# A hybrid decoder step with expert retrieval: POOL's bursts of u gathers one burst further ahead, slots in groups of two, causal key blocks, stages placed by weight

## What is computed

```python
D_MODEL, SEQ, DEC_BATCH, PAST_LEN, PAGE_SIZE = 1024, 1024, 8, 2048, 128
N_HEADS, KV_RANK, QK_ROPE, PEER_HEADS, PEER_KEYS, PEER_TOPK = 4, 256, 64, 8, 128, 16

def latent_attention(q_lat, q_rope, ckv, kr, mask):
    s = (einsum('bqhr,bkr->bhqk', q_lat, ckv) + einsum('bqhp,bkp->bhqk', q_rope, kr)) * SM_SCALE
    s = where(mask, s, -inf)                      # prompt: kpos <= qpos
    return einsum('bhqk,bkr->bqhr', softmax(s), ckv)

def peer_block(x, w_query, sub_keys, expert_u, expert_v):
    q = (x @ w_query).reshape(t, 8, 2, 128)
    s = einsum('thcd,ckd->thck', q, sub_keys)
    sv, si = top_k(s, 16)
    cand = sv[:, :, 0, :, None] + sv[:, :, 1, None, :]
    top_s, pos = top_k(cand.reshape(t, 8, 256), 16)
    experts = take(si0 * 128 + si1, pos)          # 8 x 16 = 128 experts for each token
    a = gelu(einsum('td,thkd->thk', x, expert_u[experts]))
    return einsum('thk,thkd->td', softmax(top_s) * a, expert_v[experts])
```

## Time and profile before

| | us |
|---|---|
| median of 3 runs (3758.39 to 3769.8) | 3765.8 |
| the profiled execution | 3753.85 |
| its span, first to last instruction | 3751.9 |
| first gather | 256.5 |
| tiles 0 to 6 (first u gather to the next tile's) | 403 to 416 |
| last tile, to its last v gather | 545 |

### The profile page before, as it was taken

The page is one execution under the profiler, slowest core; times in us unless marked ns, Lnnn a source line. Parts: engine busy times, 40 slices in busy tenths (PEclk is TensorE's granted clock), DMA queues, the critical chain, the costliest instruction groups (busy, mean ns, idle before and its releaser), DMA issues.

```text
span 3751.9 us, 47864 instructions
## 1 busy us (share of the span) xinstructions
...
## 2 busy tenths in 40 slices
...
GB/s 182 67 161 412 368 401 391 367 400 358 411 359 411 355 404 362 396 372 401 409 348 410 363 411 349 408 361 382 384 376 393 379 409 370 330 331 313 311 308 163
DMA packets 371757, 1321.00 MB, mean 352 GB/s; under 512 B 59684, under 2 KB 78670, under 8 KB 348424
## 3 DMA queue, kind: packets, MB, share of 16 engines
...
...
## 4 chain that ended last, share of the span: by engine, by line
PE 32%; DVE 32%; DMA 14%; issue 12%; ACT 6%; POOL 2%; SPq 1%; DVEq 1%; ACTq 0%; POOLq 0%
DVE u_ring L1310 12%; PE acc L684 11%; DMA v_ring<-in_expert_v,pick_cur 7%; PE front L410 5%; DMA u_ring<-in_expert_u,pick_cur 4%; PE front L517 3%; PE front L566 3%; PE front L538 2%; ACT diag L933 2%; DVE sv L1201 2%; PE front L518 2%; DVE si_u L1202 2%; DVE work L1201 1%; DMA w_ring<-in_w_pieces 1%; DVE work L1202 1%
## 5 line engine op out<-in xcount | busy, mean ns | idle before, releaser
L1448 POOL DMA_INDIRECT v_ring<-in_expert_v,pick_cur x1024 | 1206.2, 1178 | 687.3 <-PE acc L684 422.4
L684 PE MATMUL acc<-v_ring,diag 128*64 128x512 f32 x4096 | 1188.3, 728 | 592.4 <-ACT diag L933 419.3
L1448 POOL DMA_INDIRECT u_ring<-in_expert_u,pick_cur x1024 | 1106.7, 1081 | 666.2 <-issue 290.5
L1310 DVE CUSTOM_DVE_ANT_0 u_ring<-u_ring,xn_cur 128x1024 f32<-128x1024 f32 x1024 | 1210.6, 1223 | 268.8 <-DMA u_ring<-in_expert_u,pick_cur 253.7
L684 PEld LDWEIGHTS acc<-v_ring,diag 128*64 128x64 f32 x4096 | 348.9, 164 | 1269.2 <-issue 686.6
L410 PE MATMUL front<-work,w_ring 128*128 128x128 f32 (+1 forms) x4896 | 607.2, 283 | 7.0 <-DVE work L1194 5.6
L410 PEld LDWEIGHTS front<-work,w_ring 128*128 128x128 f32 x4896 | 593.0, 201 | 41.6 <-issue 32.6
L926 ACT ACTIVATE gelu<-dots 128x4 f32<-128x4 f32 x256 | 52.7, 206 | 1834.2 <-DVE dots L1310 1833.4
L933 ACT ACTIVATE diag<-ident,wgt 128x64 f32<-128x64 f32 x1024 | 271.5, 336 | 120.7 <-DVE wgt L1316 120.7
L566 PE MATMUL front<-w_ring,work 128*128 128x256 f32 (+1 forms) x576 | 149.7, 426 | 75.5 <-DVE work L1169 65.9
L566 PEld LDWEIGHTS front<-w_ring,work 128*128 128x128 f32 (+1 forms) x576 | 116.2, 205 | 113.3 <-issue 64.2
...
## 6 DMA issues: line engine op xcount, KB each, us to landing
...
u_ring<-in_expert_u,pick_cur POOLq DMA_INDIRECT x1024, 12.3
v_ring<-in_expert_v,pick_cur POOLq DMA_INDIRECT x1024, 10.7
...
```

Of the source, the lines that this page charges most:

```text
L684: last = nc.tensor.matmul(acc[rows, half, :], diag[:, s % RING, :], v_ring[:, s % RING, half * 512:half * 512 + 512], start=False, stop=(s ...
L1310: v.tensor_tensor_reduce(u_ring[:, slot, :], u_ring[:, slot, :], xn2_cur[:, block_of(r), :], 1.0, 0.0, ALU.mult, ALU.add, dots[:, g * G + ...
L1448: pool.indirect_dma_start(ring[:, slot, :], None, a[table][0], bass.IndirectOffsetOnAxis(ap=pick, axis=0)).then_inc(loaded[slot], 16)
```

## The change

Slots go in groups of two (G = 2, 64 groups; rings stay at 8 slots). DVE's dots and ACT's gelus run AHEAD = 2 groups ahead, four slots as before. POOL has its own bursts of 4 and issues u of burst k+2 ahead of v of burst k, over the tiles' borders. For that, selects come in parts: for tiles 1 to 7 heads 0 to 3 and 4 to 7, for tile 0 heads 0 and 1, 2 and 3, 4 to 7. Each part's picks and gates are moved at its end, except a tile's last, which is moved where before. In tile 0 only the first part stands ahead of the first gather; six queries and two selects go beside its expert part.

A table of weights (COST) places the stages: over the first 60 groups of a prompt tile, 62 of the last. Stages with several pieces of weights are split into one stage a piece. In tile 1's plan, the queries stand in groups 37 to 55, the selects in 46 and 57, and every second or third group from 17 on has no stage.

Attention covers only key blocks 0 to f in tile f. All Fori loops are unrolled; the zeroing of the key tiles by POOL is gone.

The diff, cut to its core:

```diff
...
-G = 4
+G = 2
 GROUPS = SLOTS // G
-RING = 2 * G
+RING = 8
+AHEAD = 2
+BURST = 4
 HB = P // 2
...
+def parts_of(f):
+    return [(0, 2), (2, 4), (4, 8)] if f == 0 else [(0, 4), (4, 8)]
+def parts_done(f, part):
+    return sum(len(parts_of(e)) for e in range(f)) + part
...
+_FIRST = (["norm", "turn"] + [("latent", k) for k in range(3)] + ["latent_norm"] + [("z_in", k) for k in range(2)] + ["kv_rows"]
+          + [("z_gate", k) for k in range(2)] + [("conv", k) for k in range(2)] + ["q_proj", "q_latent"])
+_MIX = ["attn", "mix_norm"] + [("mix_out", k) for k in range(N_OUT)] + ["ffn_norm", "ffn_turn", ("query", 0)]
+COST = {"norm": 0.5, "turn": 0.3, "latent": 0.5, "latent_norm": 0.8, "z_in": 0.7, "kv_rows": 0.2, "z_gate": 0.7, "conv": 0.8, "q_proj": 0.6,
...
+def _part(f, part):
+    h0, h1 = parts_of(f)[part]
+    return [("query", h + 1) for h in range(h0, h1)] + [("select", part)]
+def front_of(f):
+    return _named(_FIRST + [("head", h) for h in range(H + 1)] + _MIX + _part(f, 0))
+def rest_of(f):
+    return sum([_part(f, part) for part in range(1, len(parts_of(f)))], [])
+def place(stages, span):
+    total, done, groups = sum(COST[s[2]] for s in stages), 0.0, [[] for g in range(GROUPS)]
+    for s in stages:
+        groups[min(int(done * span / total), span - 1)].append(s)
+        done += COST[s[2]]
+    return groups
+def plan(it):
+    if it < TILES - 1:
+        stages = [(0, P) + s for s in rest_of(0)] if it == 0 else []
+        return place(stages + [(it + 1, P) + s for s in front_of(it + 1) + rest_of(it + 1)], GROUPS - 4)
+    f = it + 1
+    stages = _named(_FIRST + [("pages", n) for n in range(SB * QUARTERS + QUARTERS)] + _MIX) + _part(f, 0) + rest_of(f)
+    return place([(f, SB) + s for s in stages], GROUPS - 2)
+PLAN = [plan(it) for it in range(TILES)]
...
+def key_blocks(f, half):
+    return min(4, max(0, f + 1 - 4 * half))
...
+                    ks = slice(half * 512, half * 512 + key_blocks(f, half) * P)
+                    if ks.stop == ks.start:
+                        continue
+                    dst = F[half][:, 0:ks.stop - ks.start]
                     for c in range(2):
-                        nc.tensor.matmul(F[half][:, :], q_lat[:, c, h, :], ckvT[:, c, ks], start=(c == 0), stop=False)
-                    last = nc.tensor.matmul(F[half][:, :], q_ro[:, h, :], krT[:, ks], start=False, stop=True)
+                        nc.tensor.matmul(dst, q_lat[:, c, h, :], ckvT[:, c, ks], start=(c == 0), stop=False)
+                    last = nc.tensor.matmul(dst, q_ro[:, h, :], krT[:, ks], start=False, stop=True)
...
+                    for j in range(f + 1):
                         last = nc.tensor.matmul(F[4][:, c * P:(c + 1) * P], ckv_rows[:, j, c * P:(c + 1) * P],
-                                                W[1][:, j * P:(j + 1) * P], start=(j == 0), stop=(j == TILES - 1))
+                                                W[1][:, j * P:(j + 1) * P], start=(j == 0), stop=(j == f))
...
             def tile(it, T):
-                for g in range(GROUPS):
-                    stages = beside(g, T)
-                    before = 1 if has_pages(stages) else len(stages)
-                    for name, n in stages[:before]:
-                        stage(it + 1, T, name, n)
...
             def diag_group(it, g):
                 act.wait_ge(on.w_made, it * GROUPS + g + 1)
-                act.wait_ge(on.v_free, RING + it * SLOTS + (g - 1) * G)
+                act.wait_ge(on.v_free, it * SLOTS + (g + 1) * G)
...
+                for g in range(AHEAD + 1):
+                    gelu_group(it, g)
...
+                keys = W[0][:, 0:(f + 1) * P]
                 for half in range(2):
-                    last = v.scalar_tensor_tensor(out=W[0][:, half * 512:half * 512 + 512], in0=low_keys[:],
-                                                  scalar=small_col(C_LIM + half), in1=F[half][:, :], op0=ALU.add, op1=ALU.min)
+                    w = key_blocks(f, half) * P
+                    if w:
+                        last = v.scalar_tensor_tensor(out=W[0][:, half * 512:half * 512 + w], in0=low_keys[:, 0:w],
+                                                      scalar=small_col(C_LIM + half), in1=F[half][:, 0:w], op0=ALU.add, op1=ALU.min)
...
+            def move_gates(f, part):
+                h0, h1 = parts_of(f)[part]
+                after(dve, on.w_made, (f - 1) * GROUPS + h1 * TOPK // G if f else 0)
+                return spread_blocks(gate_cur, gate_next, h0 * TOPK // 2, h1 * TOPK // 2)
+            def move_picks(f, part):
+                h0, h1 = parts_of(f)[part]
+                after(dve, on.v_free, RING + (f - 1) * SLOTS + h1 * TOPK if f else 0)
+                spread_blocks(pick_cur, pick_next, h0 * TOPK // 2, h1 * TOPK // 2).then_inc(on.picks_moved, 1)
...
+                if T == P and (f == 0 or part < len(parts_of(f)) - 1):
+                    assert f == 0 or weighed[0] >= (f - 1) * GROUPS + hs.stop * TOPK // G
+                    own(move_gates(f, part))
+                    move_picks(f, part)
...
             def dot_group(it, g, first=0, end=G):
                 for r in range(first, end):
-                    slot = (g % 2) * G + r
-                    dve.wait_ge(u_loaded[slot], (it * (GROUPS // 2) + g // 2 + 1) * 16)
+                    s = g * G + r
+                    slot = s % RING
+                    dve.wait_ge(u_loaded[slot], (it * (SLOTS // RING) + s // RING + 1) * 16)
...
             def move_on(own, f):
-                if not isinstance(f, int):
-                    dve.wait_ge(on.w_made, f * GROUPS)
+                if f:
+                    own(move_gates(f, len(parts_of(f)) - 1))
                     dve.wait_ge(on.u_free, f * SLOTS + RING)
-                own(spread_blocks(gate_cur, gate_next, 0, HB))
                 for i in range(2):
...
+                for g, stages in enumerate(PLAN[it]):
+                    if g and g + AHEAD < GROUPS:
+                        dot_group(it, g + AHEAD)
                     if g:
                         weigh_group(it, g)
-                    before = 1 if has_pages(stages) else len(stages)
-                    for name, n in stages[:before]:
-                        stage(own, it + 1, T, name, n)
-                    if g and g + 1 < GROUPS:
-                        dot_group(it, g + 1, half, G)
-                    for name, n in stages[before:]:
-                        stage(own, it + 1, T, name, n)
+                    for s in stages:
+                        stage(own, *s)
                 if T == P:
-                    own.check(DVE_FRONT)
-                own2 = Own(dve, on.dve_peer, it * DVE_PEER + DVE_MOVE)
-                if T == P:
-                    move_on(own2, it + 1)
+                    move_on(own, it + 1)
                     dot_group(it + 1, 0)
                     total_square(it, P)
-                    dot_group(it + 1, 1)
+                    for g in range(1, AHEAD + 1):
+                        dot_group(it + 1, g)
                     weigh_group(it + 1, 0)
-                    finalize(own2, it, P)
-                    move_picks(it + 1)
-                    own2.check(DVE_PEER)
+                    finalize(own, it, P)
+                    move_picks(it + 1, len(parts_of(it + 1)) - 1)
                 else:
...
                     last.then_inc(on.state_kept, 1)
-            front.check(DVE_FRONT)
-            move_on(Own(dve, on.dve_peer, 0), 0)
-            move_picks(0)
+            move_on(own, 0)
             dot_group(0, 0)
-            dot_group(0, 1)
+            for g in range(1, AHEAD + 1):
+                dot_group(0, g)
             weigh_group(0, 0)
-            with dve.Fori(0, TILES - 1) as it:
+            for it in range(TILES - 1):
                 tile(it, P)
             tile(TILES - 1, SB)
-            own = Own(dve, on.dve_tail, 0)
...
-            pool.memset(ckv_rows[:], 0.0).then_inc(on.zeroed, 1)
-            pool.memset(ckvT[:], 0.0).then_inc(on.zeroed, 1)
-            pool.memset(krT[:], 0.0).then_inc(on.zeroed, 1)
...
-            def gather_group(it, g, table, ring, loaded):
-                if g * G == SLOTS // 2:
-                    pool.wait_ge(on.picks_moved, it + 1)
-                for s in range(g * G, (g + 1) * G):
+            def gather_burst(it, first, table, ring, loaded):
+                for part, (h0, h1) in enumerate(parts_of(it)):
+                    if first == h0 * TOPK:
+                        pool.wait_ge(on.picks_moved, parts_done(it, part + 1))
+                for s in range(first, first + BURST):
                     if table == "expert_u":
                         pool.wait_ge(on.u_free, it * SLOTS + s + 1)
...
                     waited(pool)
                     gather(table, ring, s % RING, loaded, pick_cur[:, s:s + 1])
-            def tile(it):
-                pool.wait_ge(on.picked_moved, it + 1)
-                gather_group(it, 0, "expert_u", u_ring, u_loaded)
```

(14 more changed lines are left out.)

282 lines of the change are left out of this document (124 added, 158 removed).

## The result

The changed kernel takes 4228.7 us, the median of 4 runs (4219.1 to 4235.3); the kernel before takes 3763.0. The ratio is 1.123, with a 95% interval of 1.121 to 1.126. The prediction was 3640 us, faster: wrong in sign, and 589 us off.

A forecast was written before the change was run, and what follows sets the result against it. DMA transfers, with a ceiling of 411 GB/s, were taken as the bound. Start -88, tile 0 +16, seven tiles -37, last tile -17 give -126: from 3753.9 to 3628, as a median 3640 us; range 3530 to 3735.

The forecast's parts named there:

- The start: Before the first gather: one-block attention saves 35 us, fewer queries and selects 53; first gather 88 us sooner (75 to 92).
- Tile 0: Six queries, two selects and their weights now stand beside tile 0: 16 us given back, up to 30.
- One burst further ahead: Gather order in tiles: DVE's wait for u goes, v is asked for later; costs 3 us a tile (0 to 21).
- Groups of two: In each tile: 32 more weighings on DVE, 5 us, and as many gelus on ACT; beside the work, nothing.
- Causal blocks: Attention in tiles 1 to 7: three eighths of its work goes, saving 4.3 us a tile (0 to 8).
- The change of tiles: Between tiles: first twelve u gathers wait only for free slots, loops gone; 4 of 10.4 us given back (0 to 10).
- The last tile: Last tile: weight pieces as own stages with v work between, 12 us, tile's beginning 5; saves 17 (0 to 50).
- (d): Rival: v comes too late in every zone; tiles of 433 us, 3838 us in all; chance 0.06.
- (b): Rival: order inside the tiles changes nothing, only the start gains; -82 us, 3684 in all; chance 0.17.
- (c): Rival: POOL's own pace, gathers lengthened beside DVE operations reading two tiles; tiles grow by 5 us, 3712 in all; chance 0.12.
- (a): Rival: tiles reach nearly the transfer ceiling, 388 us, DVE never starving; 3510 us in all; chance 0.25.

The follow-up runs named there:

- w1: lead1 with weighings and diagonals one group ahead and dots and gelus three groups ahead: 3636.2 us, 0.968 of the kernel before.
- g4lead1: The changed kernel with slots in groups of four again and u gathers one burst ahead, not two: 3663.8 us, 0.976 of the kernel before.
- lead1: The changed kernel with only u gathers put one burst ahead of v instead of two, groups of two kept: 3848.7 us, 1.024 of the kernel before.
- g4full: g4lead1 with attention of tiles 1 to 7 over all eight key blocks, key tiles zeroed by POOL: 3747.6 us, 0.996 of the kernel before.
- g4lead2: The changed kernel with slots in groups of four again, the lead of two bursts kept: 3803.4 us, 1.010 of the kernel before.

## Why the prediction was wrong

**What bounds the kernel** was read rightly, and the sum still failed: transfers were the limit before, at 384 GB/s, and I took for granted that they stay it. They stay it only as long as the rings are full of issued gathers. The landing time in the earlier trace rows (10.7 us against 4.7 with an empty queue) was that reserve; I used it as a range for a latency, not as the stock that the change could eat.

**The start**: right. The first gather comes at 160.1 us (forecast 168). Attention of tile 0, from its first score matmul to the first with w_uv as in the forecast's 54.9, takes 85.02 - 67.13 = 17.9 us (forecast 20), and from the end of the second query to the first gather there are 160.14 - 151.51 = 8.6 (forecast 9):

```profile
67.13 0.71 PE L557 MATMUL front<-ckvT,rows_next 128*128 128x128 f32 x4 [1.16 <-ACT rows_next L910]
...
85.02 3.78 PE L590 MATMUL front<-mo,w_uv 128*128 128x128 f32 x16 [0.46 <-ACT mo L924]
...
151.51 0.19 DVE L1294 TENSOR_TENSOR gate_next<-work 128x32 f32<-128x32 f32 x1
...
160.14 1.43 POOL L1469 DMA_INDIRECT u_ring<-in_expert_u,pick_cur  x1 [159.68 <-DVE pick_cur L1260]
```

It is -96.4 where the sum had -88. Most of the difference is that attention itself begins 7.9 us sooner (67.13 against 75.02), for which the sum had no term.

**Tile 0**: 16 us, up to 30, were to be given back beside what the other tiles do. That was too little. Before, tile 0 was 8.1 us shorter than tiles 1 to 6 (402.9 against 411.0); in the changed kernel it is 11.6 us longer than they are, so it gave back 19.7. By the same working it is 24.1 in w1, 29.6 in g4lead1, 37.1 in lead1 and 47.2 in g4full. Which of the stages beside tile 0 holds it up was not measured.

**One burst further ahead**: the step that failed most. Its loop had the right members (dots, issues, landing, PE, stage), and its sentence that v is asked for one burst later was the right one. What failed is the cover: 20.5 us of transfers for two rounds were set against a loop of 23 to 29, as if all sixteen slots could be in flight. By the count above, with dots only four slots ahead of PE's use the lead leaves 2 to 4 v slots issued, so the loop would run once for each burst, in every zone, and not in six pairs of one. I took 3 us a tile and gave 0 to 21; it is 52 (lead1 against the changed kernel), 380 us of the whole time. That DVE's wait for u would go was right, 33.4 to 13.5, and worth nothing. "The queue shortens itself when this loop binds" was true as well: landing fell to 6.7, and the loop still bound.

**Groups of two**: "beside the work, nothing" counted 32 weighings of 0.16 us and forgot what a group is in this order: the number of slots weighed before DVE goes into a stage. It is 29 us a tile (lead1 against g4lead1), 185 us of the whole, and w1 with its control shows that it is the stock and not the number of steps.

**Causal blocks**: forecast 4.3 us a tile beside the work, 0 to 8; measured 10, and 28 in tile 0. The three eighths were applied to the lost transfer time of one zone of 60 us; that attention also moves everything behind it on three engines is my reading, and no run takes it apart.

**The change of tiles**: forecast 4 of 10.4 us given back. In the changed kernel the window over it has 317 GB/s for 42 us, which is 9.6 lost; but the stop has moved. New u gathers start at once and DVE then waits for PE's last v, which stand behind them; POOL waits for the dots behind that:

```profile
1598.00:1640.00 42.00, 23.34 (x62) 6.76 (x58) 24.56 (x47) 6.69 (x20) 23.57 (x24) 0.63 0.86 317
```

```profile
1642.39 0.15 DVE L1039 TENSOR_SCALAR small<-small 128x1 f32<-128x1 f32 x1 [19.06 <-ACT acc L982]
...
1644.47 1.18 POOL L1469 DMA_INDIRECT u_ring<-in_expert_u,pick_cur  x1 [11.54 <-DVE dots L1354]
```

The 11.54 us run from 1632.9 to 1644.5, so the last 4.5 of them lie past that window. DVE's stall on the first instruction of a turn, 3.12 us, is gone from the changed kernel, as the prediction had it: at the same place, 1649.84, no time is lost. What this place gives in g4lead1 or w1 was not measured apart; g4full has it together with straight code and the new places, and there the three cost 3 us a tile instead of giving 4.

**The last tile**: forecast -17, measured +41 in the changed kernel, and +19 and +20 even in g4lead1 (562.5) and w1 (564.4). Which of its new places for stages costs that stays open.

**The rivals.** (d), v too late, was the right name with 0.06 of the chance; its 433 us a tile were 52 short, since it too kept to the zones. It said that it decides from 423 us a tile on, and lead1 (432.7) and g4lead2 (425.2) are slower than before, w1 and g4lead1 faster, as that point has it. (b), only the start gains, 3684, is near g4lead1's 3664, though not by its reason: there the tiles gain 7 us each and the rest gives it back. (c) falls: gathers take 1.03 and 1.05 us, less than before. The Trainium skill (SBUF — State Buffer, Who interferes with whom) says that a VectorE instruction with two inputs in SBUF contends with GpSimd's reads, as a dot would. The traces agree that gathers beside dots are the ones that take long (the last section has the counts), but after the change fewer do, and POOL is busy 266 us in a tile against 289. (a) is near what w1 does: 398 us and 398 GB/s in tile 3, for 388 predicted.

For the sum of what g4lead1 leaves of the change, from the profiled runs: start -94, tile 0 +22, tiles 1 to 6 -7.3 each, last tile +19, which with the tail makes 3653.6 where my sum without the two wrong steps (3 us of the loop taken out of seven tiles) would have been 3607. So the two terms of the wrong kind, the loop and the groups, carry 565 of the 589 us missed (4228.7 - 3663.8). That the rest comes so near is in part luck: the last tile is 36 us worse than its term, and causal blocks and tile 0 are both well off theirs, in opposite directions.
